# Turning a narrow expert's activation rows: one whole-array transposition or two half-array products

## The reference

```python
def swiglu(h, w_gate, w_up, w_down):
    return (jax.nn.silu(h @ w_gate) * (h @ w_up)) @ w_down

for e in range(N_EXPERTS):
    y = y + combine[..., e:e + 1] * swiglu(h, w_gate[e], w_up[e], w_down[e])
```

## Time and profile before

| | |
|---|---|
| median of 3 runs | 2416.67 us (2416.08 to 2418.52) |
| span of the profiled execution | 2415.4 us |
| mean granted TensorE clock | 0.996 |
| TensorE busy | 2368.4 us (98%) |
| VectorE busy | 935.5 us (39%) |
| ScalarE busy | 365.3 us (15%) |
| expert weights | from 1400 us on, through one queue |

### The profile page before, as it was taken

How to read it: one execution, slowest core, us unless ns; L and a number is a source line. 1 busy time by engine, 2 the same in 40 slices (tenths; PEclk the granted TensorE clock), 3 DMA queues, 4 the chain that set the end, 5 groups by cost and what they waited for, 6 DMA issues and landing times.

```text
span 2415.4 us, 30120 instructions
## 1 busy us (share of the span) xinstructions
PE 2368.4 (98%) x12002; PEld 1576.6 (65%) x12003; DVE 935.5 (39%) x1962; ACT 365.3 (15%) x988; POOL 55.4 (2%) x110
## 2 busy tenths in 40 slices
PE   9999999999999999999999999999999999999997
PEld 8956466669665666676788756699754445444553
DVE  4565233255564356755687462100211011101021
ACT  2254010012351100011000112100110010101111
POOL 0000000000000000000000000000000000000000
PEclk9999999999999999999999999999999999999999
DMA  7422343444322777454577469974999599958997
GB/s 277 149 111 97 113 173 141 152 177 167 128 81 94 270 297 299 194 194 192 227 302 308 167 247 394 424 289 186 375 422 419 206 381 421 425 231 358 417 426 295
DMA packets 78990, 617.61 MB, mean 256 GB/s; under 512 B 5984, under 2 KB 6112, under 8 KB 39184
## 3 DMA queue, kind: packets, MB, share of 16 engines
q1 hardware_dynamic: 73920, 558.39, 58.2%
q0 software_dynamic: 4656, 56.47, 5.6%
q10 hardware_dynamic: 288, 0.90, 0.1%
HBM read 614.69 MB, written 1.05 MB: 255 GB/s over the span
## 4 chain that ended last, share of the span: by engine, by line
PE 92%; DMA 4%; DVE 2%; ACT 1%; issue 1%; SPq 0%; POOL 0%; DVEq 0%; POOLq 0%; ACTq 0%
PE S L2972 9%; PE T L2592 9%; PE S L2974 8%; PE G L2331 6%; PE G L2608 5%; PE G L2986 4%; PE G L2988 4%; PE G L2363 3%; PE G L2546 3%; PE G L2871 3%; DMA big<-in_moe_pack 3%; PE S L2852 2%; PE G L2674 2%; PE T L3038 2%; PE G L2558 2%; PE G L3065 2%
## 5 line engine op out<-in xcount | busy, mean ns | idle before, releaser
L2186 DVE TENSOR_TENSOR turns<-S,turns 128x128 f32<-128x128 f32 (+2 forms) x105 | 35.5, 338 | 664.6 <-ACT turns L1280 664.6
L2972 PE MATMUL S<-big,hT 128*64 128x256 f32 x2240 | 272.1, 386 | 17.1 <-DMA big<-in_moe_pack 10.2
L2972 PEld LDWEIGHTS S<-big,hT 128*64 128x64 f32 x2240 | 157.1, 138 | 126.6 <-issue 44.2
L2592 PE MATMUL T<-hT,big 128*128 128x256 f32 x960 | 217.1, 379 | 1.1 <-ACT big L1168 1.1
L2592 PEld LDWEIGHTS T<-hT,big 128*128 128x128 f32 x960 | 182.1, 190 | 49.5 <-issue 27.7
L2974 PE MATMUL S<-big,hT 128*128 128x512 f32 x448 | 201.3, 593 | 0.3
L2974 PEld LDWEIGHTS S<-big,hT 128*128 128x128 f32 x448 | 82.8, 190 | 94.7 <-issue 94.7
L2363 PE MATMUL G<-big,hT 128*128 128x384 f32 x320 | 109.0, 490 | 0.8 <-ACT big L1058 0.8
L1285 ACT ACTIVATE pT<-T 128x128 f32<-128x128 f32 (+1 forms) x98 | 30.2, 308 | 518.9 <-PE T L2951 518.9
L2331 PE MATMUL G<-big 128*128 128x186 f32 (+1 forms) x536 | 91.8, 322 | 0.0
L2331 PEld LDWEIGHTS G<-big 128*128 128x128 f32 x536 | 86.6, 190 | 0.2
(11 more groups left out here) (500 smaller groups left out, 3494.6 us busy)
## 6 DMA issues: line engine op xcount, KB each, us to landing
big<-in_moe_pack SPq DMA_DIRECT2D x112, 2048.0 KB, 12.8
big<-in_moe_pack SPq DMA_DIRECT2D x72, 1024.0 KB, 10.0
big<-in_w_ff SPq DMA_DIRECT2D x32, 2048.0 KB, 8.0
big<-in_ada_pack POOLq DMA_DIRECT2D x24, 2048.0 KB, 12.2
big<-in_ffn_pack SPq DMA_DIRECT2D x11, 3072.0 KB, 12.7
big<-in_gate_pack SPq DMA_DIRECT2D x16, 1536.0 KB, 6.4
consts<-in_moe_pack SPq DMA_DIRECT2D x24, 1024.0 KB, 11.4
big<-in_proj_pack SPq DMA_DIRECT2D x15, 1488.0 KB, 6.4
```

The source lines that it names most:

```text
L2592: ins = mm(up_bank(c, f), w[:, k, f * P:(f + 1) * P], hT[:, k, :], start=(k == 0), stop=(k == KD - 1))
L2972: ins = mm(S[s % 2][f * FEW:(f + 1) * FEW, 0:SEQ], hTe[:, k, 0:FEW], wt[:, k, f * SEQ:(f + 1) * SEQ], start=(k == 0), stop=(k == KD - 1))
```

## The change

In `turn_hidden`, a narrow expert no longer turns its 128 columns with one transposition over the whole array. It makes two matrix products with the identity as the streamed operand: for f = 0 and 1, columns f*64 to f*64 + 64 of emsg are stationary (all 128 partitions), the 128 columns of the identity stream, and the result goes to partitions f*64 to f*64 + 64 of the same columns of T[0]. The contents of T[0] are the same up to rounding. The signal `eh_turned` goes with the second product. Experts of width 128 keep their two transpositions, and nothing else is changed.

```diff
                         pe.wait_ge(ehid_ok.sem, e * ESTEPS + (s + 3))
-                        for f in range(1 if few(w) else FT):
-                            ins = pe.transpose(T[0][:, s % 2 * SEQ + f * P:s % 2 * SEQ + (f + 1) * P], emsg[:, s % 2, SEQ + f * P:SEQ + (f + 1) * P], ident[:])
+                        for f in range(FT):
+                            if few(w):
+                                ins = mm(T[0][f * FEW:(f + 1) * FEW, s % 2 * SEQ:s % 2 * SEQ + P], emsg[:, s % 2, SEQ + f * FEW:SEQ + (f + 1) * FEW], ident[:], start=True, stop=True)
+                            else:
+                                ins = pe.transpose(T[0][:, s % 2 * SEQ + f * P:s % 2 * SEQ + (f + 1) * P], emsg[:, s % 2, SEQ + f * P:SEQ + (f + 1) * P], ident[:])
                         ins.then_inc(eh_turned.sem, 1)
```

## The result

The forecast was 2410.9 us. The changed kernel takes 2426.71 us (median of 5 runs, 2425.40 to 2431.88) against 2418.39 us of the kernel before on the same chip: 1.0037 of it, 95% interval 1.0026 to 1.0047. It is slower where a gain was forecast. A second measurement, shown last among the experiments, gave 2422.78 us, 1.0016 (1.0006 to 1.0026); it too lies outside the forecast range. All times are of undisturbed runs; one run of e2, at 4162 us and a mean granted clock of 0.555, is left out. The profiled execution has a span of 2425.7 us, 10.3 us more than before.

What follows compares the result with a forecast made beforehand. TensorE was taken to bound the kernel through the sixth expert, the weight stream the last two. Three narrow experts saving 6.1 us, less 0.27 us at the tail, gave -5.8 us from 2416.67: 2410.9 us, range 2408.5 to 2416.5.

Steps and rivals of the forecast that it cites:

- What bounds the kernel: Expert part: TensorE sets the pace through the sixth expert, the weight stream for the last two; waits for weights 10.2 us.
- The step: Narrow expert: a step falls from 5.58 to 5.39 us, as a transposition costing 0.41 us becomes products costing 0.22.
- c: Cost of the new products per turning in a narrow expert: 0.22 us, bounded between 0.11 and 0.72 us.
- (a): Rival, narrow turnings: short half-array passes run one after another with loads open, 0.72 us each; +16 us, 2433 us; chance 0.07.
- (b): Rival, narrow turnings: halves overlap but pairs stretch to 0.14 us, -3.0 us; without overlap +4.1 us; chance 0.18.
- the rule that loads of the two halves stand open: Skill rule on TensorE: weight loads overlap a running matmul only on other array rows; the halves share rows.
- the rule for transposition mode: Skill rule: transpose in transpose mode, not by matmul; alone it gives +5 us; prediction says it omits 0.30 us around it.
- The fourteenth: A narrow expert's last turning, between whole-array gather groups: the change makes it 0.46 us dearer.
- The copy's cover: ACT's copy of turned rows ahead of the down product: its free time falls from 0.32 to some 0.13 us and holds.
- The sum of -5.8 us: Whole kernel: three narrow experts save 6.1 us together, the tail behind the last weight landing loses 0.27 us.
- No wait and no DMA is added.: Work beside the path on ACT, VectorE, SyncE and transfers: the edit adds no wait and no DMA.
- Rival (d): Fifth expert's start: the edit moves the 3.46 us gap, the clock wins or loses 1.8 us; lucky clock or low cost 0.07.

Runs made afterwards that it cites:

- e2: The changed kernel with 172 never-executed instructions added behind the narrow path, against the kernel before: 2421.79 us, 1.0015.
- e9: The kernel before with 172 unused instructions ahead of the expert loop's head and 83 inside the narrow path, against the kernel before: 2417.51 us, 0.9992.
- e10: The changed kernel with 172 unused instructions ahead of the loop's head, measured beside e9, against the kernel before: 2411.61 us, 0.9970.
- e4: The layout of e2, but an expert's last turning stays a transposition, against the kernel before: 2419.86 us, 1.0000.
- e1: The kernel before with 84 never-executed instructions added behind the narrow path, against the kernel before: 2431.63 us, 1.0058.
- e6: The changed kernel with 172 unused instructions ahead of the loop's head, first run, against the kernel before: 2409.84 us, 0.9965.
- e11: The changed kernel with 171 unused instructions inside the narrow path, jumped over, against the kernel before: 2411.48 us, 0.9970.

## Why the prediction was wrong

- **What bounds the kernel: right.** No wait for a transfer ahead of the eighth expert in the changed kernel, and between e9 and e10 the stream of weights takes back 3.1 us of the 11.0 that the eighth expert starts earlier.
- **The step: right.** 5.39 us, c = 0.22 us, the four passes one behind the other without a gap. Rivals (a) and (b), that halves don't overlap or stretch, are out, and with (a) the rule that loads of the two halves stand open. Of the rule for transposition mode the prediction's reading holds: by products the turning is cheaper among half-array passes (0.22 for 0.41 us) and dearer between whole-array ones.
- **The fourteenth: right.** +0.45 us for the 0.46; e4 against e2 has it in the span, -2.2 us.
- **The copy's cover: right.** The copy ends 0.16 us ahead of the down product's first load (0.13 was forecast), and there is no wait ahead of the down product in the chain of the step.
- **The sum of -5.8 us: right as the change's own worth within what was measured** (-5.9 us, uncertain by some 3.6, e10 against e9; -4.9 and -8.9, the two measurements against e1), wrong as a forecast of this kernel. By the trace the four experts ahead of the eighth gain 9.5 us where 8.1 were reckoned, and the eighth loses 3.1 where 2.3 were: 6.4 for 5.8; the other 1.5 us of the 8.0 between the spans lie ahead of the first expert, which the change doesn't touch. In rival (a) the constant is 15.4, not 15.3, by its own terms; nothing hangs on it.
- **The step that failed: "No wait and no DMA is added."** I went through semaphores, copies and weight transfers, and not through the instructions themselves. 84 more of them in one path move all that lies behind, and the jump back of the 128-column path went over a block boundary. It then took 6.73 and 6.07 us for 0.47, which made the two 128-column experts 6.3 and 5.6 us longer; e1 shows the same without the change. The profile of before had the sign of it: I cited the 3.46 us of "issue" in the earlier trace rows and took it in rival (d) as a fixed gap that only moves, without asking what TensorE's stream waited for. The line of the compare at L649, 5.04 us, would have told.
- **Rival (d), the clock: its size was too small.** I allowed 1.8 us, at the gap ahead of the fifth expert. The fall in the wide expert's last passes cost 6.6 us in one execution and was missing in another. It is not what made the forecast fail: the second measurement, without it, is 2422.78 us.
- **The range** ended at break-even and held no case in which the change pays for itself and the program around it loses.

The order of sizes in the end: layout +11.9 us, clock 0 or +6.6, the change -5.9. A version that beats both kernels is the change in another place: 0.9965 and 0.9970 (e6, e10), 0.9970 (e11).

Open remain which block is dropped for another, what selects the executions in which the clock falls with TensorE busy, and whether leaving the fourteenth turning to the transposition gains anything that a measured time can show.

## What to carry to other kernels

Where a program has loops and paths chosen at run time, count what an edit adds to the code, and look at every taken jump behind it: its duration in the trace, which block it lies in, and which block its target lies in. Idle time put down to "issue" at a jump is a cost that can be removed or doubled by placement alone, so an edit that changes code size is judged against the kernel before padded to the same layout. In this program a path's start wants to be in the block of the jump that precedes it and not in the last few slots of it.

## What was not expected of the hardware

- A jump or compare whose block of instructions isn't loaded takes 4.6 to 6.8 us on TensorE here, and running over into such a block leaves it idle for 1.5 to 3.8 us; around those of some 6 us and more the clock was granted at 0.50 for 6.8 to 10.2 us. Some jumps and compares at the start and the end of the wide expert and at the end of the last took 1.4 to 3.9 us; what sets them apart was not followed.
- The granted clock fell to 0.50 for 13.65 us with TensorE busy all the time, in passes of which every second one uses 16 rows of the array, and in the next execution of the same program it did not.
- 84 instructions that are never executed make the kernel 0.58% slower (e1), and 172 elsewhere, with 83 more to jump over, don't (e9: 0.9992).
